# Two RMS norms: squares of seven chunks added on VectorE, their sum and the last chunk reduced on TensorE

## The reference

```python
def rms_norm(x, g, eps=1e-6):
    xf = x.astype(jnp.float32)
    y = xf * lax.rsqrt(jnp.mean(xf * xf, axis=-1, keepdims=True) + eps)
    return (y * g.astype(jnp.float32)).astype(x.dtype)
...
        h = h + merged @ w_out[l]
        u = rms_norm(h, norm_ffn[l])
        gate_ff, up_ff = jnp.split(u @ w_ffn_in[l], 2, axis=-1)
...
        x = x + gate1 * (merged @ w_out[l])
        h2 = rmsnorm(x, norm2_w[l]) * (1.0 + scale2) + shift2
        x = x + gate2 * hierarchical_moe(h2, w_rg[l], b_rg[l], w_re[l], b_re[l],
                                         w_gate[l], w_up[l], w_down[l])
```

## Time and profile before

| | us |
|---|---|
| median of 3 runs | 1708.03 (1707.67 to 1709.07) |
| the profiled execution | 1713.64 |
| its span in the trace | 1711.8 |
| PE busy | 1600.1 (93% of the span) |
| PE weight loads busy | 1208.1 (71%) |
| DVE busy | 812.0 (47%) |
| ACT busy | 541.1 (32%) |
| POOL busy | 83.7 (5%) |
| mean granted clock of PE | 0.968 of full speed |

### The profile page before, as it was taken

The page is one execution under the profiler, slowest core; times in us unless marked ns, Lnnn a source line. Parts: engine busy times, 40 slices in busy tenths (PEclk is TensorE's granted clock), DMA queues, the critical chain, the costliest instruction groups (busy, mean ns, idle before and its releaser), DMA issues.

```text
span 1711.8 us, 20145 instructions
## 1 busy us (share of the span) xinstructions
PE 1600.1 (93%) x8255; PEld 1208.1 (71%) x8255; DVE 812.0 (47%) x1402; ACT 541.1 (32%) x878; POOL 83.7 (5%) x107
## 2 busy tenths in 40 slices
PE   7999999999999999999998999999999994888775
PEld 6987777777788788888885787797678882333332
DVE  6556344454364866675214963436652624222111
ACT  5334453444444222222113423331453321111110
POOL 5000000000000000000000010000000001121111
PEclk9999999999999999999999999989999996999998
DMA  5335121221323466663322232221124617999994
GB/s 162 112 99 143 57 74 50 74 74 61 88 95 116 135 195 221 221 198 122 98 87 59 83 116 79 69 74 50 50 75 148 221 78 292 401 411 402 406 410 179
DMA packets 147088, 260.45 MB, mean 152 GB/s; under 512 B 16584, under 2 KB 121332, under 8 KB 133680
## 3 DMA queue, kind: packets, MB, share of 16 engines
q1 hardware_dynamic: 138544, 241.41, 40.0%
q0 software_dynamic: 8448, 17.70, 3.7%
HBM read 253.79 MB, written 15.25 MB: 157 GB/s over the span
## 4 chain that ended last, share of the span: by engine, by line
PE 84%; DVE 7%; issue 4%; ACT 2%; DMA 2%; POOL 0%; POOLq 0%; DVEq 0%; ACTq 0%
PE psum L2369 20%; PE psum L2370 19%; PE psum L2371 19%; PE psum L2927 7%; PE psum L2944 4%; PE psum L2667 1%; PE psum L2656 1%; PE psum L2639 1%; PE psum L2905 1%; DMA Xg<-h_rows,tok 1%; DVE cst L1934 1%; DVE WL L1507 1%; PE psum L2566 1%; PE psum L2436 1%; ACT Sb L1066 1%
## 5 line engine op out<-in xcount | busy, mean ns | idle before, releaser
L2369 PE MATMUL psum<-AHs,WH 128*128 128x512 f32 x744 | 306.6, 412 | 8.3 <-DVE WL L1507 4.7
L1507 DVE TENSOR_TENSOR WL<-raw,WH 128x2048 fp32r<-128x2048 f32 (+1 forms) x100 | 226.7, 2267 | 181.2 <-ACT WH L981 180.8
L2371 PE MATMUL psum<-AHs,WL 128*128 128x512 f32 x744 | 293.7, 395 | 0.0
L2370 PE MATMUL psum<-ALs,WH 128*128 128x512 f32 x744 | 293.2, 394 | 0.0
L981 ACT ACTIVATE WH<-raw 128x2048 fp32r<-128x2048 f32 (+1 forms) x100 | 189.0, 1890 | 139.9 <-PE psum L2371 107.7
L2369 PEld LDWEIGHTS psum<-AHs,WH 128*128 128x128 f32 x744 | 141.9, 191 | 44.4 <-issue 6.1
L2369 PE MATMUL psum<-AH,WH 128*128 128x512 f32 (+1 forms) x464 | 169.4, 365 | 0.0
L2370 PE MATMUL psum<-AL,WH 128*128 128x512 f32 (+1 forms) x464 | 164.2, 354 | 0.0
L2370 PEld LDWEIGHTS psum<-ALs,WH 128*128 128x128 f32 x744 | 141.9, 191 | 31.0 <-issue 3.1
L2371 PEld LDWEIGHTS psum<-AHs,WL 128*128 128x128 f32 x744 | 141.6, 190 | 30.9
L2371 PE MATMUL psum<-AH,WL 128*128 128x512 f32 (+1 forms) x464 | 163.3, 352 | 0.0
(11 more groups left out here) (534 smaller groups left out, 2306.6 us busy)
## 6 DMA issues: line engine op xcount, KB each, us to landing
raw<-w_in SPq DMA_DIRECT2D x45, 1024.0 KB, 5.2
WE<-w_gate SPq DMA_DIRECT2D x34, 1024.0 KB, 22.0
WE<-w_up SPq DMA_DIRECT2D x34, 1024.0 KB, 24.6
WE<-w_down SPq DMA_DIRECT2D x34, 1024.0 KB, 24.9
araw<-w_ada SPq DMA_DIRECT2D x24, 1024.0 KB, 5.5
raw<-w_ffn_in SPq DMA_DIRECT2D x22, 1024.0 KB, 7.9
raw<-w_ffn_out SPq DMA_DIRECT2D x11, 1024.0 KB, 4.9
raw<-w_out SPq DMA_DIRECT2D x8, 1024.0 KB, 5.1
```

The source lines that it names most:

```text
L1507: V.tensor_tensor(WL[:, n, 0:w], raw[:, n, 0:w], WH[:, fed[0] % HL, 0:w].bitcast(F32), ALU.subtract).then_inc(S_("lo_ready"), 1)
L2369: MM(dst, lh, rh, start=first, stop=False)
L2370: MM(dst, lh, rl, start=False, stop=False)
L2371: return MM(dst, ll, rh, start=False, stop=last)
```

## The change

In the first norm DVE adds the squares of chunks 1 to 6 one after the other onto chunk 0 in `merged`: chunk 1 at the end of slab wo 1, chunks 2 and 3 at the end of slab 2, chunks 4, 5 and 6 at the end of slab 3, each time behind the two `ALu` instructions. `norm_sums` is called once, where the call for the last two chunks was: PE takes the sum of seven chunks and then chunk 7, 4 products each. The three calls at the ends of slabs are gone.

In the second norm DVE adds chunk by chunk too (`square_added`), behind the slab's `feed` and ahead of its first evacuation; chunk 6 comes ahead of the evacuation of chunk 7. `sq2` has the same four places, with place 0 kept for the sum. `rows_of(c)` waits for the updated chunk of `hT` instead of its square and keeps router product and transposes; its sums remain for c = 7 alone, 8 products ahead of the router's. In both norms together 16 products stand where 64 stood, and 12 additions of 128x512 are new on DVE. The cut diff:

```diff
@@ sync
                     if n == 0:
-                        sp.wait_ge(*when("n_ffn_summed", KC))
+                        sp.wait_ge(*when("n_ffn_summed", 2))
@@ scalar, end
                         if k == "wo2" and c >= 4:
-                            act.wait_ge(*when("n_two_summed", c - 3))
-                        sq = merged[:, c, :] if k == "wo" else sq2[:, c % 4, :]
+                            act.wait_ge(*when("n_two_added", c - 3))
+                        sq = merged[:, c, :] if k == "wo" else square_at(c)
@@ vector, evacuate
+                        n = g[1]
+                        if k == "wo2" and n == KC - 1:
+                            square_added(KC - 2)
                         src = ready(g)
-                        n = g[1]
@@ vector
+            def square_added(c):
+                dve.wait_ge(*when("n_two_squared", c + 1))
+                if c > 1:
+                    dve.wait_ge(*when("n_two_added", c - 1))
+                V.tensor_tensor(square_at(0), square_at(0), square_at(c), ALU.add).then_inc(S_("n_two_added"), 1)
@@ vector, end
+                    for c in range(max(1, 2 * name[1] - 2), KC - 1 if name[1] == 3 else 2 * name[1]):
+                        dve.wait_ge(*when("n_ffn_squared", c + 1))
+                        if c > 1:
+                            dve.wait_ge(*when("n_ffn_added", c - 1))
+                        V.tensor_tensor(merged[:, 0, :], merged[:, 0, :], merged[:, c, :], ALU.add).then_inc(S_("n_ffn_added"), 1)
@@ vector, walk over the slabs
                     begin(s)
+                    if s["name"][0] == "wo2":
+                        for c in range(max(1, 2 * s["name"][1] - 2), 2 * s["name"][1]):
+                            square_added(c)
                     evacuate(s, s["outs"])
@@ tensor
-            def norm_sums(n0, n1):
-                for n in range(n0, n1):
-                    pe.wait_ge(*when("n_ffn_squared", n + 1))
-                    for t in range(NB):
-                        ins = MM(bank(4, 1, t), merged[:, n, P * t:P * t + P], ones[:, 0:1], start=n == t == 0,
-                                 stop=n == KC - 1, skip_group_check=True)
-                    ins.then_inc(S_("n_ffn_summed"), 1)
+            def norm_sums():
+                pe.wait_ge(*when("n_ffn_added", KC - 2))
+                for t in range(NB):
+                    ins = MM(bank(4, 1, t), merged[:, 0, P * t:P * t + P], ones[:, 0:1], start=t == 0, stop=False, skip_group_check=True)
+                ins.then_inc(S_("n_ffn_summed"), 1)
+                pe.wait_ge(*when("n_ffn_squared", KC))
+                for t in range(NB):
+                    ins = MM(bank(4, 1, t), merged[:, KC - 1, P * t:P * t + P], ones[:, 0:1], start=False, stop=True,
+                             skip_group_check=True)
+                ins.then_inc(S_("n_ffn_summed"), 1)
@@ tensor, rows_of
-                pe.wait_ge(*when("n_two_squared", c + 1))
-                for t in range(NB):
-                    ins = MM(bank(4, 1, t), sq2[:, c % 4, P * t:P * t + P], ones[:, 0:1], start=c == t == 0, stop=c == KC - 1,
-                             skip_group_check=True)
-                ins.then_inc(S_("n_two_summed"), 1)
+                freed(pe, ("wo2", c))
+                if c == KC - 1:
+                    pe.wait_ge(*when("n_two_added", KC - 2))
+                    for t in range(NB):
+                        MM(bank(4, 1, t), square_at(0)[:, P * t:P * t + P], ones[:, 0:1], start=t == 0, stop=False, skip_group_check=True)
+                    pe.wait_ge(*when("n_two_squared", KC))
+                    for t in range(NB):
+                        ins = MM(bank(4, 1, t), square_at(c)[:, P * t:P * t + P], ones[:, 0:1], start=False, stop=True,
+                                 skip_group_check=True)
+                    ins.then_inc(S_("n_two_summed"), 1)
@@ tensor, end
-                if k == "wo" and name[1]:
-                    norm_sums(2 * name[1] - 2, 2 * name[1])
@@ tensor, walk over the slabs
                         if s["name"] == ("ffg", 0) and j == 0:
-                            norm_sums(KC - 2, KC)
+                            norm_sums()
```

More of the change, by code:

```diff
@@ L326, in shared_events @@
     families = [
-        ("norm", [("n_ffn", dict(norm, **split)), ("n_fin", norm), ("n_one", dict(bc=1, **mean, **split)),
+        ("norm", [("n_ffn", dict(norm, **dict(split, summed=2))), ("n_fin", norm), ("n_one", dict(bc=1, **mean, **split)),
                   ("mn", dict(squared=C1, summed=C1, bc=C1, **mean)),
-                  ("dn", dict(squared=C1, summed=C1, bc=C1, **mean)), ("n_two", dict(squared=KC, summed=KC, **mean))]),
+                  ("dn", dict(squared=C1, summed=C1, bc=C1, **mean)), ("n_two", dict(squared=KC, summed=1, **mean))]),
         ("merge", [("m1", dict(oh=3 * C1, ol=3 * C1, merged=2 * KC, hi=KC, lo=KC)),
@@ L493, in build_program, with square_at @@
         sq2 = at("sq2", W0, [4, S])
+        def square_at(c):
+            return sq2[:, (c - 1) % 3 + 1 if c else 0, :]
         WE = [at(f"WE{n}", kb, [KC * 2 * DE + 2 * D]) for n, kb in enumerate((159.8125, 183.8125, 135.8125, 35, 59, 83))]
@@ L837, in _ @@
             load_expert(sp, 2, 0, 2)
-            sp.wait_ge(*when("n_two_summed", KC))
+            sp.wait_ge(*when("n_two_summed", 1))
             load_expert(sp, 2, 1, NE // 2 + 2)
@@ L1623, in first_ffn @@
                 feed(h + 1)
-                dve.wait_ge(*when("n_ffn_summed", KC))
+                dve.wait_ge(*when("n_ffn_summed", 2))
                 V.tensor_scalar(stat[:, 40:44], bank(4, 4), 1.0 / D, EPS, ALU.mult, ALU.add).then_inc(S_("n_ffn_ms"), 1)
@@ L2183, in _ @@
                     begin(s)
+                    if s["name"][0] == "wo2":
+                        for c in range(max(1, 2 * s["name"][1] - 2), 2 * s["name"][1]):
+                            square_added(c)
                     evacuate(s, s["outs"])
                     end(s)
-            dve.wait_ge(*when("n_two_summed", KC))
+            dve.wait_ge(*when("n_two_summed", 1))
             V.tensor_scalar(stat[:, 40:44], bank(4, 4), 1.0 / D, EPS, ALU.mult, ALU.add).then_inc(S_("n_two_ms"), 1)
```

## The result

| | before | change |
|---|---|---|
| median beside each other (8 runs each) | 1708.55 (1704.69 to 1712.98) | 1699.28 (1697.37 to 1703.03) |
| the profiled execution | 1713.64 | 1698.56 |
| its span | 1711.8 | 1696.6 |
| PE busy | 1600.1 | 1581.3 |
| DVE busy | 812.0 | 819.4 |

What follows compares the result with a forecast made beforehand. PE was taken as the bound, busy for 93% of the span. First norm 1.68 us off plus second norm 5.46 make 7.14, so from 1708.03 the forecast was 1700.9 us, range 1698.4 to 1704.2.

Steps and rivals of the forecast that it cites:

- Slab ends of wo 1 and wo 2: First norm: two calls removed from PE's stream with nothing in their place, 2 x 1.79 = 3.58 us off.
- The third call turns into a wait: End of slab wo 3: PE idles 1.92 us at ffg 0 for DVE's additions; second half starts 0.23 us later.
- The clock: Behind the wait at ffg 0 the granted clock falls to half, costing 1.67 us; first norm 1.68 us off.
- The rival that the clock stays up: First norm: no fall of the granted clock, 8.81 us off in all, 1699.2 us; chance 0.28.
- Second norm, no wait in rows_of: Chunk 4's delayed evacuation ends near 1380.3, PE comes at 1381.5; 1.2 us to spare, so no cost.
- Second norm, 7 x 0.80 = 5.60: In rows_of the sums of chunks 0 to 6 go, 0.80 us each from a gapless stream, 5.60 us off.
- The end: Behind the last dense slab, the added row of sums brings PE to the router's loads 0.14 us later.
- Nothing I take out is part of that: The profiled execution's 5.6 us above the median holds nothing removed, so 7.14 us comes off 1708.03.
- The expert stage: Rival: shifted start puts one or two pairs at half clock, 1704.1 or 1707.3 us; chance 0.08.
- slower: Rival: in the expert stage one pair's weights land late, PE loses 13.7 us, 1714.6 us; chance 0.03.
- the cheap products: Rival: both norms' removed products cost less than their pace, only 2.5 us gained, 1705.5 us; chance 0.01.
- second norm for nothing: Rival: PE isn't the bound in the second norm, which gives nothing, 1706.4 us; chance 0.02.

Runs made afterwards that it cites:

- The repeat: The change run again unaltered against the kernel before: 1700.78 us beside 1708.02, ratio 0.9954, 7.9 us less.
- The early additions: The change with the first norm's additions placed behind the next slab's feed, ahead of its evacuations: 1694.38 us (0.9921) against before, in a second set 1694.57 (0.9923).
- the first norm alone: The kernel before with only the wo part of the diff: 1705.93 us, ratio 0.9983, 2.9 us less.
- the filled wait: The change with eight unread wide products in PE's wait at ffg 0, against before: 1700.97 us (0.9944), run again 1697.16 (0.9948).
- the second profile: The kernel before, unchanged, profiled a second time: 1707.30 us, span 1705.5.
- the first profile of before: The kernel before, unchanged, in its original profiled execution: 1713.64 us, span 1711.8.
- the second norm alone: The kernel before with only the wo2 part of the diff: 1703.69 us, ratio 0.9966, 5.8 us less.
- third profile: The kernel before, unchanged, profiled a third time: 1707.19 us, span 1705.4.
- the sums twice: The kernel before with the second norm's sums for chunks 0 to 6 issued a second time into unread columns: 1722.17 us in one run.

## Why the prediction was right and wrong

The direction came out, and so did the mechanisms that the sum is built on: products taken out of a gapless stream, a third call that turns into a wait, a fall of the clock behind it. One term was too small, 7 x 0.80 for the rows of sums, and the time read beside before, 1697.6, lies 0.8 us below the range. With that term right the forecast would have been 1700.4, so most of the 3.3 us between 1700.9 and 1697.6 isn't the term's. The repeat, 7.9 us less, gives 1700.1 and all runs together, 8.9, give 1699.1, both inside the range: part of the miss is the luck of one comparison, and some 1.3 us stays open.

- **Slab ends of wo 1 and wo 2.** As forecast: nothing takes the calls' place, 1.79 us each. The early additions, where no wait is left, show 1.79 for all three calls (5.38 for 5.37).
- **The third call turns into a wait.** As forecast: 1.89 us for 1.92, released by the third addition. The rule that let it be forecast is the count of what stands ahead on DVE.
- **The clock.** Taken as the likelier with 1.67; the fall came, in all three traces with that wait (the change twice, the first norm alone), and in none of those without it. Its size by the filled wait is 1.53 to 1.67. The first norm as a whole: 1.60 off for 1.68. The rival that the clock stays up is out by these traces, although its 8.81 us stand nearer to the 8.9 of all runs than the forecast's 7.14.
- **Second norm, no wait in rows_of.** Right; chunk 4's evacuation ran at 1369.98 and PE came at 1371.92.
- **Second norm, 7 x 0.80 = 5.60.** This step failed by size. The distance from the first sum to the router's first product is what a row of eight costs as the first behind a wide product. Once it is gone the router's row becomes the first and takes 0.81 where it took 0.90. The right price is the difference of two spacings, with and without: 0.89, so 7 x 0.89 = 6.23 off. The end gave back 0.23 (chunk 7's update to the router 2.61 for 2.38 in the second profile) where 0.14 was forecast, since the new row there is a further one too. The second norm gives 6.0 for 5.46.
- **The end.** In the first profile of before the router's products for chunk 7 ran at half clock and in the third in part; in the second they ran at full, as in every trace of the change. From there to the end the three take 306.59, 304.46 and 305.89 us, the change 304.27. So the stretches above, which go by the second profile, count 0.2 us there, and against the other two it would be 1.6 and 2.3. The last is over the 2 us that the prediction set as a sign of a wrong step in the expert stage, and it is a difference of clock between profiles of one kernel as much as of the change.
- **"Nothing I take out is part of that" and a range down to 1698.4.** This failed most. The range took the median of three runs, 1.4 us apart, as exact and left 0.8 us below its cases. 55 runs of before lie between 1703.3 and 1713.1. Within one kernel the time goes with the granted clock: the second norm alone took 1697.3 us in an execution at 0.98 and 1704 to 1706.9 at 0.969 to 0.972. So one comparison of eight runs a side can stand 1 to 3 us from the stretches' sum, as 10.4 against 7.6 does.
- **The expert stage, slower, the cheap products, second norm for nothing.** Out: chunk 7 to the end is no longer than in any profile of before; an instruction with one column costs 0.11 us with its load; the second norm alone gives 5.8 us. The Trainium skill (TensorE: Matmul & The Clock Gate, section LDWEIGHTS (loading the stationary operand)) puts a load at P/1.2 ns for P columns, for 128 columns 107 ns as an estimate. The pace in the trace, 0.89 / 8 = 0.111 us, agrees with it; the 0.19 us that the trace records for one such load does not.

**What stays open.** The stretches give 7.6 us, all runs 8.9 ±1.3. One candidate for the rest is the clock at the router's products for chunk 7, which the change does touch. A fall reached them in three of the five traces with the end of before (its first and third profile, the sums twice) and in none of the six with the change's end. From the first of these products to the end the five take 304.5 to 306.6 us, 305.5 in the mean, and the six 304.1 to 304.5, 304.2 in the mean. That is 1.3 us, as much as is missing, but the fall isn't there each time and no run was made to bring it on or keep it away. Another candidate is the clock behind hsqd. It fell there in all four traces with the second norm's sums on PE and the first norm's calls in place (three of before, the sums twice; 1.5 us in the second profile: 70.00 against 68.46 with the first norm alone, which has the same sums for chunk 0). It fell in none of the eight traces with either part of the change, where hsqd to the router takes 67.6 us (68.46 there). But with the second norm alone PE's stream up to that point is that of before, and its part of the change stands 60 us later. No run tells what would cause this. Neither candidate is shown, and neither is counted as the change's; the second norm alone had neither fall in its trace, and its runs show no surplus over its stretches (6.0 us, ±2.1).

## What to carry to other kernels

Price a row of small products by the spacing of its wide neighbours with and without it, not by the distance to what follows, and count each addition that takes its place on the engine where it queues: moved from the end of the slab to ahead of its evacuations, so that the last was done 3.3 us before PE asked for it, the same additions gave some 4 us more (3.8 in the stretch, 4.9 between the means), which is the version to keep. A short wait followed by one-column products can cost the clock behind it on top of itself, here 1.5 us for a wait of 1.9, and so can a longer run of small products without any wait: the doubled sums cost 6.4 us of clock beside their own 5.3. And where runs of one kernel spread by several us with the granted clock, read more than one profile of it before a range of a few us is given.

## What the runs showed of the hardware

- The eight instructions of a row of small products (4 products in fp32) take 0.81 us behind a wide product and 0.89 to 0.90 behind another such row, whether the moving side has 1 or 36 columns.
- PE idle for 1.89 us and then 1.85 us of one-column products had the granted clock at half right behind them; the same products behind 1.98 us of wide work did not.
- Small products without a gap can have it too: in the kernel with the sums twice three rows ran from 1354.00 without a wait, and the granted clock stood at half from 1356.6. The same rows from 1361.41 had none.
- The same instructions on PE had a fall of the clock in one kernel (0.50 at 1287.3 of the second profile of before) and none in another (1.00).
- One execution of 4246.78 us, with PE slow from the start, among all runs of this study.
